# Gated-linear-attention output products taken two banks at a time: 128-row products first, 64-row products behind them

## What is computed

```python
q_dec  = q * exp(b)                                  # b: running sum of log gates in the chunk
scores = where(causal, q_dec @ (k * exp(-b)).T, 0)   # within the chunk
o_intra = scores @ v
u       = (k * exp(b_last - b)).T @ v                # per chunk
S_n     = exp(b_last) * S_{n-1} + u                  # the recurrence, 64 x 128 per head
o_inter = q_dec @ S_{n-1}
o       = o_intra + o_inter
```

## Time and profile before

| | us |
|---|---|
| median of 3 runs | 2137.47 |
| lowest, highest run | 2137.01, 2144.78 |
| the profiled execution's own time | 2137.27 |
| span of the profiled execution, first to last instruction | 2135.5 |
| TensorE busy in the span | 2075.6 (97%) |
| VectorE, ScalarE, GpSimd busy | 1413.8, 959.9, 275.5 |

### The profile page before, as it was taken

One profiled execution on the slowest core, in us unless ns is written; L12 is line 12 of the kernel. 1 busy time (PEld: TensorE's weight loads), 2 busy tenths in 40 slices (PEclk: granted clock), 3 DMA queues, 4 the chain that ended last, 5 costly groups with the idle time before them and its releaser, 6 DMA issues.

```text
span 2135.5 us, 38907 instructions
## 1 busy us (share of the span) xinstructions
PE 2075.6 (97%) x16332; PEld 2015.7 (94%) x16332; DVE 1413.8 (66%) x1983; ACT 959.9 (45%) x1494; POOL 275.5 (13%) x250
## 2 busy tenths in 40 slices
PE   5999999999999999999999999999999999999996
PEld 5999999998889899999989999999888889999996
DVE  6768577544547867658886775864545488675774
ACT  5535254232553635435463543532335446353551
POOL 1100001300113100000310000031020130000004
PEclk9999999999999999999999999999999999999998
DMA  6655463221313456646344654522231236454542
GB/s 181 160 148 159 136 167 103 92 71 59 116 62 119 132 155 163 174 119 163 114 130 138 162 152 116 154 80 88 74 126 59 79 108 161 123 157 139 149 108 72
DMA packets 99453, 265.10 MB, mean 124 GB/s; under 512 B 16336, under 2 KB 16384, under 8 KB 99280
## 3 DMA queue, kind: packets, MB, share of 16 engines
q1 hardware_dynamic: 75152, 200.65, 28.6%
q0 software_dynamic: 24128, 61.97, 14.8%
HBM read 255.28 MB, written 11.44 MB: 125 GB/s over the span
## 4 chain that ended last, share of the span: by engine, by line
PE 89%; DVE 7%; ACT 2%; DMA 1%; issue 0%; SPq 0%; DVEq 0%; ACTq 0%
PE pu L690 25%; PE px L768 22%; PE pu L768 22%; PE px L690 12%; PE px L940 2%; DVE wl L1395 1%; PE px L907 1%; PE px L918 1%; DVE zl L1468 1%; PE px L883 1%; PE px L889 1%; DMA raw<-in_w_out 1%; PE pu L717 1%; DVE zf L1449 0%; DVE zxl L1463 0%
## 5 line engine op out<-in xcount | busy, mean ns | idle before, releaser
L1037 ACT ACTIVATE wh<-raw 128x1024 fp32r<-128x1024 f32 (+1 forms) x116 | 118.0, 1017 | 343.2 <-PE pu L690 224.0
L690 PE MATMUL pu<-zh,wh 128*128 128x272 f32 x1056 | 231.4, 300 | 4.7 <-DVE wl L1395 3.7
L582 POOL DMA_DIRECT2D raw_y<-in_gate_up x88 | 77.0, 875 | 1195.5 <-DMA raw_y<-in_gate_up 1195.5
L690 PE MATMUL pu<-zh,wl 128*128 128x272 f32 x1056 | 218.5, 288 | 0.0
L690 PE MATMUL pu<-zl,wh 128*128 128x272 f32 x1056 | 217.9, 288 | 0.0
L1395 DVE TENSOR_TENSOR wl<-raw,wh 128x1024 fp32r<-128x1024 f32 (+2 forms) x140 | 171.7, 1227 | 48.9 <-ACT wh L1037 39.0
L690 PEld LDWEIGHTS pu<-zh,wh 128*128 128x128 f32 x1056 | 164.1, 188 | 25.8 <-issue 16.6
L690 PEld LDWEIGHTS pu<-zl,wh 128*128 128x128 f32 x1056 | 165.9, 188 | 0.0
L690 PEld LDWEIGHTS pu<-zh,wl 128*128 128x128 f32 x1056 | 165.1, 189 | 0.0
L1412 DVE TENSOR_TENSOR wl<-raw,wh 128x1024 fp32r<-128x1024 f32 x88 | 109.4, 1244 | 57.7 <-ACT wh L1060 57.4
L1060 ACT ACTIVATE wh<-raw 128x1024 fp32r<-128x1024 f32 x88 | 93.2, 1059 | 111.8 <-PE pu L768 39.1
(11 more groups left out here) (279 smaller groups left out, 6541.7 us busy)
## 6 DMA issues: line engine op xcount, KB each, us to landing
raw<-in_gate_up SPq DMA_DIRECT2D x88, 512.0 KB, 4.4
raw_y<-in_gate_up SPq DMA_DIRECT2D x88, 512.0 KB, 3.9
raw_y<-in_gate_up POOLq DMA_DIRECT2D x88, 512.0 KB, 5.7
raw<-in_down SPq DMA_DIRECT2D x64, 512.0 KB, 3.8
raw<-in_w_in SPq DMA_DIRECT2D x50, 512.0 KB, 3.4
raw_q<-in_gate_up SPq DMA_DIRECT2D x88, 256.0 KB, 3.7
raw<-in_down SPq DMA_DIRECT2D x32, 384.0 KB, 3.9
raw<-in_w_out SPq DMA_DIRECT2D x16, 512.0 KB, 3.5
```

What stands on the lines that cost most here:

```text
L582: pool.dma_start(raw_y[b % 2][:, :, :], gate_up[layer, i, mat, 1].rearrange("p (t c) -> p t c", t=2), accum_op=ALU.add).then_inc(y_summed[ ...
L690: mm = pe.matmul(out[:, a, 0:HALF], w[slot][:, k * P:(k + 1) * P], z[:, k, a * HALF:(a + 1) * HALF], start=(first and n == 0), stop=(last ...
L1037: act.activation(unit_hi[slot][0:rows, 0:columns], raw_of(("unit", U))[0:rows, 0:columns], ACT.Copy)\
```

## The change

Within `gla_out` the loops are exchanged. For `t` 0 the 128-row products of both parities are issued one behind the other, each into its own bank, and then the four 64-row products of both parities; then the same for `t` 1. The waits for a parity's bank and scores stand ahead of its first 128-row product, so those of parity 1 now come before the 64-row products of parity 0. Each bank is reported finished behind its last product, as before. No product, no operand and no bank is different.

```diff
-                    for par in range(2):
-                        d = slice(A_DK * par, A_DK * par + A_DK)
-                        out = use(layer, ("O", tt, par))
-                        wait_for(pe, dve_free, layer, ("AT", tt, par))
-                        for t in range(2):
+                    for t in range(2):
+                        cols = slice(t * A_DV, (t + 1) * A_DV)
+                        for par in range(2):
                             h = 2 * t + par
-                            cols = slice(t * A_DV, (t + 1) * A_DV)
-                            pe.matmul(out[0:rows, cols], atm[0:rows, tt % 2, par, t, 0:rows],
+                            if t == 0:
+                                use(layer, ("O", tt, par))
+                                wait_for(pe, dve_free, layer, ("AT", tt, par))
+                            pe.matmul(bank(use_no[("O", tt, par)])[0:rows, cols], atm[0:rows, tt % 2, par, t, 0:rows],
                                       av[0:rows, tt, h * A_DV:(h + 1) * A_DV],
                                       start=True, stop=False, skip_group_check=True)
+                        for par in range(2):
+                            d = slice(A_DK * par, A_DK * par + A_DK)
+                            out = bank(use_no[("O", tt, par)])
                             for c in range(2 if tt < NTT - 1 else 1):
                                 ...
                                 mm = pe.matmul(out[i, cols], aqkT[d, t, t0 + i.start:t0 + i.stop], before,
                                                start=False, stop=True, skip_group_check=True)
-                        mm.then_inc(*pe_out.of(("O", tt, par)))
+                            if t == 1:
+                                mm.then_inc(*pe_out.of(("O", tt, par)))
```

## The result

The changed kernel takes 2126.84 us (median of six runs, 2125.47 to 2128.67). The kernel before, run beside it, gives 2138.92 over its six runs. The ratio is 0.9941, with a 95% interval of 0.993 to 0.9952. Forecast were 2126.8 us and a gain of 10.5, with 0.60 for a change within 0.5% and 0.38 for more; the ratio is 0.59%, and its interval lies across that bound.

A forecast was written before the change was run, and what follows sets the result against it. TensorE, busy 97% of the span, was taken to bound the kernel. From 2137.27 us, 8.8 for eight prompt tiles' O steps and 1.7 for the sample tile's came off, giving 2126.8 us; range 2125.9 to 2131.3.

The forecast's parts named there:

- The bound: TensorE, busy 97% of the span with one wait from 466 to 640 us; O-step savings are kernel time.
- The second 128-row product: In each half of a prompt tile's O step, following one of its own shape: 0.22 us more, at most 0.33.
- the rule that I weighed: Rival: the second 128-row product in the same row group pays an uncovered 0.11 us load; 1.8 us, 2128.6, chance 0.04.
- Four 64-row products: In each half of a prompt tile's O step, both row halves run together: 0.38 us a set, priced from U.
- the other end: Rival: row halves take turns, 0.58 us per set of four instead of 0.38; 4.0 us, time 2130.8, chance 0.08.
- The sample tile: Its O step goes from 2.65 to 1.80 us, 0.85 less; two layers give 1.7 us.
- The moved wait: Parity 1's wait for VectorE's keys' copy comes sooner, 0.24 us left at the fourth prompt tile; costed at nothing.
- ScalarE's two copies: Both now come at the O step's end, the state store 0.37 us later against TensorE; costed at nothing.
- The gain given back: Rival: behind the side units a weight load meets more traffic, 3.2 us a layer, 6.4 in all; 2133.2, chance 0.03.
- The scatter of 0.5: Allowance in us at both ends of the forecast range, like that between the lowest and the middle run.
- a bound of 10.7: The gain in us that makes 0.5%, about what a measurement can tell from no change; the forecast stops just short.

The follow-up runs named there:

- e1: Against the change: parity is the outer loop, each parity's two 128-row products, then its four 64-row ones in one row half; 2130.23 us, ratio 0.9964.
- e4: Against the change: VectorE copies the next tile's keys twice, so the bank that parity 1 needs comes free later; 2128.12 us, ratio 0.9953 of before.
- e5: Against the change: all four 128-row products, then all eight 64-row ones, and each tile's U directly behind the previous tile's O step; 2120.47 us, 0.9915 of before.

## Why the prediction was right, step by step

**The bound.** That TensorE's own time in the `O` steps is the kernel's time held: 10.52 us less in the ten steps (4 x 1.096 + 0.877 a layer), 10.45 less in the two stretches.

**The second 128-row product**, 0.22 from the other head group's run: 0.53 where one product had taken 0.31, and 0.64 for 0.42. Right, though the run that gave the price moves 64 columns a product (128x64 in the earlier trace rows) and these move 128; the prediction went by the shape of the weights alone. The weight loads show why that was enough. In that run eight of them span 0.97 us (first row, kernel before), in the pair of the change four span 0.54 (second row), so that they follow each other 0.11 apart in both, two to a product:

```profile
548.81 0.97 PEld L940 LDWEIGHTS px<-bv,pt 128*128 128x128 f32 x8
491.36 0.54 PEld L883 LDWEIGHTS px<-av,atm 128*128 128x128 f32 x4
```

This also decides for these products against the rule that I weighed, from the Trainium skill, page "TensorE: Matmul & The Clock Gate", section "The mechanism": an uncovered load of 0.11 does not show, though both products use the same rows.

**Four 64-row products**, 0.38 from `U`: 0.38. e1 showed what the other end would have been, 0.58, and it was forecast as such.

**The sample tile**, 1.80 forecast, 1.78 measured.

**The moved wait** had 0.24 us left at the fourth tile, as worked out, and e4 shows that this was the tile to look at. How far the waits moved was misread: in the earlier trace rows parity 1 begins at 492.87, 1.46 us behind the step's start and not 1.57, so its waits come 1.24 us sooner and not 1.36. The 0.24 does not hang on it.

**ScalarE's two copies** at the end of the step cost TensorE nothing, as costed: no wait for them in its rows, and the stretch gained what the steps did.

**The gain given back** behind the side units did not come, as the load of 6.20 us and the span show.

**What was less right.** The mechanism held term by term; that the time fell within 0.04 us of the forecast is luck. The sum starts from 2137.27, 1.65 below the 2138.92 of the kernel before in these runs, and the medians differ by 1.6 more than forecast, and the two cancel. The scatter of 0.5 in the range was too small as well: the lowest of the six runs of the change is 1.4 below their median. Then the chances. A sum of 10.5 against a bound of 10.7 is a toss, and I gave 0.60 to the side where the measured ratio is not. The ratio is further from 1 than the traces make it: 12.1 us between the medians, 10.45 in the stretches. The kernel before ran at 2137.01 to 2144.78 in those six runs, with 2138.92 in the middle where the three that I had seen gave 2137.47. All five experiments show the same sign, medians 0.4 to 1.9 us further from before than their stretches. I cannot tell from these runs whether that is before's own scatter, to which its runs above 2140 point, or a real microsecond outside the stretches; the traces, one of each, don't show one. It stays open.

## To carry to other kernels

Where small products of several shapes are put between large ones, count the changes of array shape on the engine's timeline, and measure one from the distance between starts: here a 128-row and a 64-row part cost 0.78 us a time, of which the passes of the products themselves are 0.44, twice 0.22. Group by shape as far as the waits allow, also across steps that have nothing to do with one another, and put products of different row halves and banks side by side. Ahead of such a regrouping, look for the wait that moves forward and at which tile its cover is thinnest.

## What the runs showed of the hardware that was not expected

A change from 64 to 32 rows costs like a change of shape although both are smaller than the array. The sample's step shows it already, and the prediction priced it so: 0.33 us from product to product in the earlier trace rows, and with the change 0.55 for a pair of one shape, 0.22 for the second. What e5's expectation had left open is whether it holds for `U`. It does: in e5 the sample's `U` came 0.11 us later behind eight 64-row products than the 64-row `U` did (0.60 and 0.49 us).
